# Bias rows loaded as contiguous runs, attention scores issued two pairs ahead behind the preceding pair's values, and query rows turned later, in a four-block float32 transformer kernel

## The reference

```python
for l in range(2):                       # first kind
    h = rmsnorm(x, norm_mix_pre[l]); proj = h @ w_in[l]
    ya = global_axial_attention(...)     # A: 8 query heads, 2 key heads of 64, softmax over all 512 keys
    yb = pool_mixer(...)                 # windowed means of 2, 4, 8, 16 tokens, four 128x128 products
    yc = neighbourhood_attention(...)    # C: 8 heads of 64, 8 x 16 window of an 8 x 64 grid, bias rpb
    merged = sum(sigmoid(gate) * (y @ w_branch)); x = x + rmsnorm(merged @ w_out[l])
    x = x + rmsnorm(conv_gated_mlp(rmsnorm(x), ...))
# second kind: block 3 is a 31-tap convolution module and an MLP;
# block 4 is a dilated attention (D: 3 window groups x 8 heads of 128) with its own query norm gain,
# keys and values from kv_norm(x), and an MLP
```

## Time and profile before

| | |
|---|---|
| device time, median of 3 (lowest, highest) | 3315.86 us (3313.65, 3316.2) |
| profiled execution, device time | 3318.09 us |
| its span, first to last instruction | 3316.3 us |
| mean granted TensorE clock | 0.986 |
| TensorE busy | 3167.2 us (96%) |
| VectorE, ScalarE busy | 1688.1 us (51%), 1198.9 us (36%) |
| DMA | 285.03 MB, mean 86 GB/s |

### The profile page before, as it was taken

One profiled execution on the slowest core, in us unless ns is written; L12 is line 12 of the kernel. 1 busy time (PEld: TensorE's weight loads), 2 busy tenths in 40 slices (PEclk: granted clock), 3 DMA queues, 4 the chain that ended last, 5 costly groups with the idle time before them and its releaser, 6 DMA issues.

```text
span 3316.3 us, 42241 instructions
## 1 busy us (share of the span) xinstructions
PE 3167.2 (96%) x17113; PEld 2608.9 (79%) x17113; DVE 1688.1 (51%) x2228; ACT 1198.9 (36%) x1612; POOL 159.4 (5%) x171
## 2 busy tenths in 40 slices
PE   5989999999989899999999889999899999999999
PEld 5766888888877588888887568888788888788887
DVE  3465455553444744565527855552543534555543
ACT  2444224342333622444323254442322212344432
POOL 3030000000021200000002110000000000000000
PEclk8999999999999999999999999999999999999999
DMA  6121323322342032332322123223221121222222
GB/s 144 58 68 52 96 94 102 101 90 93 100 86 74 26 102 89 102 101 94 101 96 78 52 67 104 89 95 102 84 89 64 64 89 62 70 92 96 94 89 89
DMA packets 230545, 285.03 MB, mean 86 GB/s; under 512 B 5156, under 2 KB 188492, under 8 KB 230412
## 3 DMA queue, kind: packets, MB, share of 16 engines
q1 hardware_dynamic: 225628, 266.89, 24.9%
q0 software_dynamic: 4784, 16.24, 2.3%
HBM read 281.02 MB, written 2.10 MB: 85 GB/s over the span
## 4 chain that ended last, share of the span: by engine, by line
PE 83%; DVE 10%; ACT 3%; issue 2%; DMA 1%; POOL 0%; DVEq 0%; SPq 0%; ACTq 0%; POOLq 0%
PE ps L1566 18%; PE ps L1567 18%; PE ps L1568 18%; PE ps L1679 6%; PE ps L1681 6%; PE ps L1680 6%; DVE t_wlo L1022 2%; ACT t_whi L664 2%; DMA t_wraw<-in_w_in_dram 1%; PE ps L1605 1%; PE ps L1604 1%; PE ps L1603 1%; DVE t_vb L1486 1%; PE ps L2098 1%; DVE t_x L1067 1%
## 5 line engine op out<-in xcount | busy, mean ns | idle before, releaser
L1022 DVE TENSOR_TENSOR t_wlo<-t_wraw,t_whi 128x2048 fp32r<-128x2048 f32 x252 | 579.7, 2300 | 1324.8 <-ACT t_whi L664 1324.8
L1566 PE MATMUL ps<-t_hh,t_whi 128*128 128x512 f32 (+1 forms) x2704 | 1012.9, 375 | 14.6 <-DVE t_accv L1216 5.1
L1567 PE MATMUL ps<-t_hl,t_whi 128*128 128x512 f32 (+1 forms) x2704 | 1003.8, 371 | 0.0
L1568 PE MATMUL ps<-t_hh,t_wlo 128*128 128x512 f32 (+1 forms) x2704 | 1003.7, 371 | 0.0
L664 ACT ACTIVATE t_whi<-t_wraw 128x2048 fp32r<-128x2048 f32 x252 | 482.6, 1916 | 1385.8 <-PE ps L1568 962.3
L1566 PEld LDWEIGHTS ps<-t_hh,t_whi 128*128 128x128 f32 x2704 | 511.8, 189 | 116.7 <-issue 17.0
L1567 PEld LDWEIGHTS ps<-t_hl,t_whi 128*128 128x128 f32 x2704 | 512.0, 189 | 88.0 <-issue 2.4
L1568 PEld LDWEIGHTS ps<-t_hh,t_wlo 128*128 128x128 f32 x2704 | 511.7, 189 | 87.3
L1679 PE MATMUL ps<-t_whi,t_midh 128*128 128x512 f32 x704 | 274.4, 390 | 0.0
L1681 PE MATMUL ps<-t_whi,t_midl 128*128 128x512 f32 x704 | 274.0, 389 | 0.0
L1680 PE MATMUL ps<-t_wlo,t_midh 128*128 128x512 f32 x704 | 273.9, 389 | 0.0
(11 more groups left out here) (277 smaller groups left out, 3728.8 us busy)
## 6 DMA issues: line engine op xcount, KB each, us to landing
t_wraw<-in_w_in_dram SPq DMA_DIRECT2D x46, 1024.0 KB, 5.3
t_wraw<-in_w_up_dram SPq DMA_DIRECT2D x44, 1024.0 KB, 5.1
t_wraw<-in_ffn_w_in_dram SPq DMA_DIRECT2D x44, 1024.0 KB, 5.1
t_wraw<-in_w_kv_dram SPq DMA_DIRECT2D x24, 1024.0 KB, 5.2
t_wraw<-in_w_down_dram SPq DMA_DIRECT2D x20, 1024.0 KB, 5.1
t_wraw<-in_ffn_w_out_dram SPq DMA_DIRECT2D x20, 1024.0 KB, 5.0
t_wraw<-in_w_branch_dram SPq DMA_DIRECT2D x12, 1024.0 KB, 5.0
t_wraw<-in_w_q_dram SPq DMA_DIRECT2D x12, 1024.0 KB, 5.1
```

Of the source, the lines that this page charges most:

```text
L1022: v.tensor_tensor(wlo[slot][:, :], wraw[slot][:, :], whi[slot][:, :].bitcast(F32), ALU.subtract).then_inc(w_lo, 1)
L1566: te.matmul(out, wh, xh, start=first, stop=False)
L1567: te.matmul(out, wh, xl, start=False, stop=False)
L1568: return te.matmul(out, wl, xh, start=False, stop=last)
```

## The change

Four parts, all in one diff. The bias rows are loaded as one contiguous run of 3534 floats for each partition, and in layer 0 this waits for the end of the first norm's split. In `pair_attention` scores run two pairs ahead: TensorE issues scores(j+2) behind weigh(j-1), and VectorE takes both maxima of pair j+2 ahead of divide(2j+2), with one scaling for two. C's probabilities get four slots. A's first scores are issued between the two tiles of the second `pu` chunk, whose split work moves to the end of A, and the first merge chunk's first tile stands ahead of A's last weighing. In D the query rows are turned and split around the first two chunks, and head pair 0 does key and value chunks first.

```diff
-            rpb_rows = sb("rpb_rows", 120 * 32, stack=s)
+            rpb_rows = sb("rpb_rows", 120 * 31, stack=s)
...
-                pC = sb("pC", SLOTS * T, stack=u)
-                cmask = sb("cmask", 2 * WIN, stack=u)
+                pC = sb("pC", 4 * T, stack=u)
...
-        D_ORDER = [(kD, vD, qD), (kD, vD, qD), (kD, qD, vD)]
+        D_ORDER = [[(kD, 0), (vD, 0), (kD, 1), (vD, 1), (kD, 2), (qD, 0), (qD, 1), (qD, 2), (vD, 2)]]
+        D_ORDER += 3 * [[(kD, 0), (vD, 0), (qD, 0), (kD, 1), (vD, 1), (qD, 1), (kD, 2), (qD, 2), (vD, 2)]]
...
+                if l == 0:
+                    pool.wait_ge(h_lo, SPLIT["pre0"] + 8)
                 for r in range(ROWS_C):
 
-                    src = bass.AP(tensor=A["rpbp"].tensor, ap=[[1, 16], [31, 113], [1, 32]],
+                    src = bass.AP(tensor=A["rpbp"].tensor, ap=[[1, 16], [1, 114 * 31]],
                                   offset=RPB_PAD + (l * 8 * 15 + r) * 31 - 8)
-                    pool.dma_start(rpb_rows[16 * r:16 * r + 16, 0:113 * 32].rearrange("p (r k) -> p r k", k=32),
-                                   src).then_inc(rpb_in, 16)
+                    pool.dma_start(rpb_rows[16 * r:16 * r + 16, 0:114 * 31], src).then_inc(rpb_in, 16)
...
+            def pair_maxima(n0, j, scores_in, factors):
+
+                q = (n0 + 2 * j) % 4
+                for n in (2 * j, 2 * j + 1):
+                    dve.wait_ge(scored, n0 + n + 1)
+                    ins = scores_in(n, (n0 + n) % 4, q + n % 2)
+                    if not factors:
+                        ins.then_inc(maxed, 1)
+                if factors:
+                    ch.link(ins)
+                    v.tensor_tensor(small[:, q:q + 2], small[:, 4 + q:6 + q], factors(2 * j), ALU.mult).then_inc(maxed, 2)
...
-                    if j == 0 and j in extra:
-                        extra[j]()
+                    if j == 0:
+                        if j in extra:
+                            extra[j]()
+                        pair_maxima(n0, 1, scores_in, factors)
+                    if j < pairs - 2:
+                        pair_maxima(n0, j + 2, scores_in, factors)
                     if j < pairs - 1:
-                        negated_max(n0, 2 * j + 2, scores_in, scale)
-                        negated_max(n0, 2 * j + 3, scores_in, scale)
                         divide(n0 + 2 * j + 2, pbuf, T)
...
-                pair_attention("C", STEPS[f"C{l}"], pC, {3: lambda c=c: hi(c + 5)})
+                pair_attention("C", STEPS[f"C{l}"], pC, {7: lambda c=c: hi(c + 5)})
...
+                between[0] = second_pu
+                between[16] = lambda c=c: hi(c + 1)
...
+                scores(1)
                 for j in range(pairs + 1):
-                    if j < pairs - 1:
-                        if j:
-                            pe.wait_ge(probs if kind == "A" else maxed, n0 + 2 * j)
-                        scores(j + 1)
                     if j < pairs:
                         turn_probs(n0, 2 * j, pbuf)
...
                         weigh(j - 1)
+                    if j < pairs - 2:
+                        pe.wait_ge(probs if kind == "A" else maxed, n0 + 2 * j + 2)
+                        scores(j + 2)
                     if j < pairs:
                         turn_probs(n0, 2 * j + 1, pbuf)
...
-                start(c + 1, d=d + 1)
-                rows_out(c + 1, (hh, hl), bank0=0).then_inc(w_used, 1)
-                pe.wait_ge(head_std, 2 * l + 2)
-                pe.wait_ge(qk_ready, 6 * l + 6)
-                pe.wait_ge(drained, 2 + d + 2)
...
+                row_tile(c + 1, (hh, hl), 0, bank(4))
+                pe.wait_ge(head_std, 2 * l + 2)
+                pe.wait_ge(qk_ready, 6 * l + 6)
                 scores_a(0)
+                row_tile(c + 1, (hh, hl), 1, bank(5)).then_inc(w_used, 1)
...
+                def first_gate(c=c, d=d):
+                    start(c, d=d)
+                    row_tile(c, (hh, hl), 0, bank(6))
...
-            d_chunk(0, 0, 1)
-            pe.wait_ge(h_lo, SPLIT["hq"] + 2)
+            d_chunk(0, 1)
+            pe.wait_ge(h_lo, SPLIT["hq"] + 4)
             turn_row("hq", 2, 2)
-            pe.wait_ge(h_lo, SPLIT["hq"] + 4)
             turn_row("hq", 3, 3)
+            d_chunk(0, 2)
+            d_chunk(0, 3)
+            d_chunk(0, 4)
             pe.wait_ge(h_lo, SPLIT["hq"] + 8)
-            d_chunk(0, 0, 2)
```

More of the change, by code:

```diff
@@ L559, in _ @@
                     for s in range(2):
[L560 to L568, removed]
+                        for i in range(2):
+                            for h in range(2):
+                                at = (2 * hp + s) * 15 * 31 + (8 if i else 16 * h)
+                                rows = rpb_rows[:, at:at + ROWS_C * 31].rearrange("p (r k) -> p r k", k=31)[:, :, 0:16]
+                                to = (2 * i + h) * P
+                                ins = gp.tensor_tensor(
+                                    e2[hp][:, 2 * s * WIN + to:2 * s * WIN + to + P].rearrange("p (r k) -> p r k", k=16),
+                                    cmask[:, to:to + P].rearrange("p (r k) -> p r k", k=16), rows, ALU.subtract)
                     ins.then_inc(e2_ready, 1)
@@ L917, in _, with pu_rows, second_pu @@
                 W = T + 2 * PAD
-                for j in range(2):
-                    hi(c + j)
+                def pu_rows(j, b, W=W):
                     sc.activation(pu[:, 2 * j * W:2 * (j + 1) * W].rearrange("p (m w) -> p m w", m=2)[:, :, PAD:PAD + T],
[L921 to L924, removed]
+                                  bank(b, 2).rearrange("p (m w) -> p m w", m=2), ACT.Copy).then_inc(pu_in, 1)
+                def second_pu(c=c):
+                    act.wait_ge(w_used, c + 2)
+                    pu_rows(1, 4)
+                hi(c)
+                pu_rows(0, 2)
+                act.wait_ge(head_sum, 5 * l + 5)
+                sc.activation(rq[:, 0:32], bank(5)[:, 0:32], ACT.Sqrt, bias=epsc).then_inc(head_std, 1)
                 def pooled_hi(g, l=l):
@@ L1116, in hand_over @@
                 row_lo(pre, hh, hl, 3)
[L1117 to L1123, removed]
             def divide(g, pbuf, width):
-                q, s = g % 4, g % SLOTS
+                q, s = g % 4, g % (4 if pbuf is pC else SLOTS)
                 dve.wait_ge(probs, g + 1)
@@ L1529, in _, with qkv_out @@
[L1529 to L1534, removed]
+                def qkv_out(i, hp=hp, c=c):
+                    lo(c + i)
+                    dst, g = D_ORDER[hp][i]
+                    b0, b1 = d_banks(hp, i)
+                    for h, b in enumerate((b0, b1)):
+                        if dst is vD:
+                            ins = v.tensor_copy(vD[:, :].rearrange("p (b g n) -> p b g n", b=4, g=3)[:, 2 * h:2 * h + 2, g, :],
+                                                bank(b).rearrange("p (b n) -> p b n", b=2))
+                        else:
+                            ins = v.tensor_copy(tile(dst, 2 * g + h), bank(b))
+                    ins.then_inc(drained, 1)
@@ L1535, in _ @@
+                if hp == 0:
+                    scale_row("hq", 0)
+                    scale_row("hq", 1)
+                for i in range(8):
+                    qkv_out(i)
+                    if hp == 0 and i < 2:
+                        row_lo("hq", qh, ql, 2 * i, 2)
+                        row_lo("hq", qh, ql, 2 * i + 1, 3)
+                        if i == 0:
+                            scale_row("hq", 2)
+                            scale_row("hq", 3)
+                c += 9
                 n0 = STEPS["D"] + 8 * hp
@@ L1766, in turn_probs @@
                 g = n0 + n
+                slots = 4 if pbuf is pC else SLOTS
                 pe.wait_ge(scaled, g + 1)
@@ new lines, in gate_rows, with branch_rows @@
+                def gate_rows(n, g, j, c=c, d=d):
+                    cc = c + 3 * g + j
+                    if isinstance(n, int):
+                        start(cc, d=d + 3 * g + j)
+                    else:
+                        start(cc, n, 6, d + 3 * g + j)
+                    rows_out(cc, (hh, hl), bank0=6 - 2 * j).then_inc(w_used, 1)
+                def branch_rows(n, g, c=c, d=d):
+                    cc = c + 3 * g + 2
+                    if isinstance(n, int):
+                        start(cc, d=d + 3 * g + 2)
+                    else:
+                        start(cc, n, 6, d + 3 * g + 2)
+                    for t in range(4):
+                        for k in range(4):
+                            at = k * 512 + t * P
+                            ins = mm3(bank(t), whi[cc % 2][:, at:at + P], wlo[cc % 2][:, at:at + P],
+                                      tile(yh, n * 4 + k), tile(yl, n * 4 + k), k == 0, k == 3)
+                    ins.then_inc(w_used, 1)
```

145 lines of the change are left out of this document (69 added, 76 removed).

## The result

The changed kernel takes 3331.97 us (median of 6, 3326.41 to 3332.94), the kernel before 3316.03 (median of 6). The ratio is 1.0043 [1.0031, 1.0055]: 0.43% slower, where the prediction had 3300.5 us. The profiled execution of the changed kernel is its fastest of the six, 3326.41 us with a span of 3324.6, so the two traces show 8.3 us of the 15.9.

The account below looks back on a forecast made before the run. TensorE, busy 96% of the span, bounds the kernel. Start -21, layer 1's bias loads -7.8, D -8.7, C +4, A +18 make -15.5 us: profiled 3302.6, median about 3300.5, forecast's range 3290 to 3309, overall 3284 to 3317.

Parts of the forecast that it names:

- A: Attention stage A, both layers: scores two pairs ahead lose 9 us a layer, 18 in all, bounds 11 and 27.
- layer 1's bias tables: Layer 1's bias loads as contiguous runs: TensorE's wait for `t_vrows` mostly goes, 7.8 us gained, bounds 0 and 7.8.
- The start: Program start, bias rows behind the first norm: weight products start at about 21.3 instead of 42.4, about 21 us gained.
- D: Stage D: TensorE's 6.32 us wait before the query chunk and its clock loss go, 8.7 us gained, bounds 6.3 and 9.5.
- C: Attention stage C, both layers: 2 us lost a layer, 4 in all, bounds 0 and 8.
- the loop: Both attentions: scores, maxima, division, turn, weighing close a cycle through TensorE and VectorE, 5.0 us a pair or 5.1.
- the bias tables cost nothing: GpSimd's 32 table operations, both layers: 17.2 to 34.4 us, done before they are needed, costed at nothing.
- the rival of slow loads: Bias loads: runs into one partition stay slow, layer 1 gains nothing, layer 0 stalls 7.8 us; 3316 us, chance 0.11.
- 13 rings: Attention stage A, each layer: 13 passes of the loop at 5.0 us bring scores 15, bounds 4.75 and 5.35 a pass.
- The clock rival: Both attentions: TensorE's clock falls to half in the loop's pauses, 2.5 us a ring, 3345 us with half; chance 0.08.
- The first rival: Both attentions: two pairs ahead really works ahead, a pair costs 3.3 us, 62 us together, about 3238 us; chance 0.07.

Follow-up runs that it names:

- e1: Changed kernel with VectorE doing divide(2j+2) ahead of the maxima of pair j+2: 3255.35 us, ratio to before 0.9811.
- e4: Changed kernel with the second half of layer 1's GpSimd table operations waiting for VectorE's weight-chunk split: 3325.51 us (median of 12).
- e6: Changed kernel with the pool mixer's GpSimd operations cut to 8 of 512 columns, windowed means left out: 3323.65 us (median of 12).
- e5: Changed kernel with the edits of e1 and e4 together: 3247.86 us, ratio to before 0.9792.
- e10: e5 with scores(j+2) ahead of weigh(j-1) on TensorE and layer 0's table operations in three parts: 3244.16 us, ratio to before 0.9778.
- e3: Changed kernel with scores only one pair ahead on TensorE and VectorE, as before, still one scaling for two: 3285.08 us, ratio to before 0.9903.

## Why the prediction was wrong

The forecast was 15.5 us gained and the two traces show 8.3 us lost. Of these 23.8 us, A in two layers has 14.5, layer 1's bias tables 7.0 and block 3 3.7; the rest nearly cancels.

**Right.** The start (20.2 of 21), D (8.6 of 8.7), C (1.8 and 2.0 of 2), the loop and its length: 4.97 and 5.07 us where 5.0 and 5.1 were worked out from hand-over times of a trace that has no such loop. e1 shows that this loop is the cost: opened at one place, it gives back 77 us. Two positions of that working aren't in the earlier trace rows. They stand in the timeline of the kernel before:

```profile
276.57 0.66 PE L1772 MATMUL ps<-t_base,t_pA 128*128 128x128 f32 x4
...
284.05 1.09 PE L1808 MATMUL ps<-t_gain,t_vA 128*64 128x128 f32 x16 [0.69 <-ACT t_gain L788]
```

**Wrong: the bias tables cost nothing.** "I cost them at nothing; the cover is the three chunks ahead of C." The step asked only whether the tables are due in time, which they are by 29 us in layer 1. It didn't ask who else uses what GpSimd uses. The wait for the bias rows did go (in layer 1 the next split starts 9.0 us earlier than before, against 4.2 one split earlier), and VectorE's held split took 4.0 of these 4.8 us back. The term measured 0.8 instead of 7.8; e4 gives the rest back. This is neither the forecast nor the rival of slow loads: issuing the 8 takes 3.84 us instead of 7.85, and all is there at 921.89, ahead of the split.

**Mis-sized: A, 14.2 and 18.3 us instead of 9.** 13 rings at 5.0 us were right for the steady ones, and the forecast left out two things that the traces show. The first is VectorE's stretched operations. In the first two pairs of each layer the scores reach the turn that waits in 4.50 and 5.13 us (layer 0) and 4.50 and 6.08 us (layer 1) instead of 3.37. Less 0.1 and 0.95 us for scores at half clock that is 2.8 and 2.9 us; e6 removes this stretch, and layer 1's first pairs are 4.97 there. The second, and the larger, is the clock. Summed over the turns, weighings and scores that took longer than in a steady pair, it comes to about 2.9 us in layer 0 and 6.8 in layer 1 (estimates from the timeline). Together that is 15.4 us, and 1.3 go off again, since the ring is 4.97 and a product 0.87. Some of the half clock lies in the first pairs (windows above), some in the last of layer 1:

```profile
1150.51 2.08 PE L1981 MATMUL ps<-t_kA,t_qA 64*128 64x512 f32 x4
...
1155.41 1.53 PE L1840 MATMUL ps<-t_gain,t_vA 128*64 128x128 f32 x16
1156.87 1.97 PE L1802 MATMUL ps<-t_base,t_pA 128*128 128x128 f32 x8
```

**The rivals.** The clock rival was given 0.08 and is at work beside the forecast's loop, with 9.7 of the 14.5 us that A has too much. In the profiled execution eight of the 36 rings have a granted clock of 0.69 to 0.94, two have 0.97 and 0.99, and 26 have 1.00; in e6's eleven have 0.76 to 0.90. In e1 and e5, without this loop, the clock is 1.00 over the same stages, so here the half clock came with the loop's pauses; what decides which ring loses it isn't shown. The rival was priced at 2.5 us a ring; a slow pair of C costs 1.2 to 1.5, because only the weighing and the scores slow down and the turns around the wait do not. The argument against it, D's attention at 2.86 of 5.00 us and a clock of 1.00, showed one loop that kept its clock and not that all do. The Trainium skill (TensorE: Matmul & The Clock Gate, What's actually happening) has half clock as the default state, released by activity; the eight rings agree with it, and 26 with the same work and the same pauses kept 1.00. The first rival's price holds, 3238 us forecast and 3244 measured once both engines' orders allow it (e10), but the order as changed forbids it.

**Open.** Of the 15.9 us by the medians the traces leave 7.6: the changed kernel's median is 5.6 us above its profiled execution, and the kernel before's 2.1 below its own. The clock is the likely cause, but no trace of a slower execution exists. In e4, which has the loop, the executions of 3318.5 to 3318.8 us have a mean clock of 0.992 to 0.993 and those above 3329 us 0.988 to 0.989. The spread alone says little: the executions of the changed kernel span 6.5 us and those of e4 12, but those of the kernel before, without the loop, span 12 too, in 22 executions. The 3.7 us in block 3 lie in its convolution, whose streams are unchanged and whose waits are nearly the same; of its twelve windows of 5 us seven are below 1.00 after and three before. The same stretch is 2.7 us longer than before in e3's trace and as long as before in e6's, and nothing here says why.

## What to carry to other kernels

Here issuing work earlier on one in-order engine lost time, because its consumer on the other was put ahead of something that the first engine needed sooner. Draw the cycle through both streams, and through the buffer slots, and count how many iterations it spans. An operation moved off the critical path isn't free if it shares hardware with one that lies on it: ask of GpSimd's work which VectorE operation runs at that time.

## What the hardware showed unasked

A VectorE split of two SBUF tiles beside back-to-back GpSimd operations of 0.4 us took 7.6 to 8.8 us in all six profiled executions of layer 1 with 32 of them in a row, each time held until the last was done, not until the one that was running was. In layer 0 the same pair took 2.4 to 2.6 us in six executions, with one GpSimd operation stretched from 0.43 to 2.48 us instead, and 9.8 to 10.3 in three. With 16 operations of twice the size it took 2.80 before. Which of the two waits differed between executions in layer 0 and was always VectorE in layer 1. What the Trainium skill (SBUF — State Buffer, SBUF: two separate sides) says of one instruction's hold does not cover this row of them. VectorE's maxima, which read the scores from PSUM, kept their 1.29 us beside the pool mixer's work on GpSimd.
